# The down-projection of a two-layer encoder as seven block products, and the conv norm's transposes regrouped

## The chip, the core and the metric

The program runs on one core of a Trainium2 chip. Its metric is the device time of one execution in microseconds. The engines of the core run their own instruction streams and meet at semaphores: TensorE (PE, with weight loads shown as PEld), VectorE (DVE), ScalarE (ACT), GpSimd (POOL), and SyncE (SP), which here only issues transfers. ACT issues transfers too.

## What is computed

Two layers work on 1,024 prompt tokens and 256 sample tokens of width 1,024, all in float32. Layer 0 mixes tokens by a convolution module, layer 1 by windowed attention; each is followed by a gated feed-forward block of inner width 2,752 (21 tiles of 128 and a rest of 64):

```python
def conformer_conv(x, w_pw1, b_pw1, w_dw, b_dw, g_n, b_n, w_pw2, b_pw2):
    h = x @ w_pw1 + b_pw1
    a, gate = jnp.split(h, 2, axis=-1)
    h = depthwise_conv(a * jax.nn.sigmoid(gate), w_dw, b_dw)
    h = jax.nn.silu(layer_norm(h, g_n, b_n))
    return h @ w_pw2 + b_pw2
...
def conv_ffn(x, w_up, w_dw, b_dw, w_down):
    h = depthwise_conv(x @ w_up, w_dw, b_dw)
    g, u = jnp.split(h, 2, axis=-1)
    return (jax.nn.silu(g) * u) @ w_down
...
    for i in range(DEPTH):
        x = layer_norm(DEEPNORM_ALPHA * x + mix(x), ln_mix_g[i], ln_mix_b[i])
        x = layer_norm(DEEPNORM_ALPHA * x + conv_ffn(x, ...), ln_ffn_g[i], ln_ffn_b[i])
```

## The kernel before

The 1,280 tokens are ten row tiles of 128 (0 to 7 prompt, 8 and 9 sample). Every operand of a matrix product is split into a high and a low part, and `product` (L816) issues three matmuls for each product: high x high, low x high, high x low. Weights come in pieces of 128 rows and 512 columns: SP loads one into one of four slots of `raw_pieces`, ACT copies its high part into one of eight slots of `w_hi` once PE has used the piece eight before it, POOL subtracts to get the low part (`low`, L716), and only then is the raw slot free for SP.

The up-projection of the prompt already works by seven block products. It runs 21 sections (`sections`, L1072), one for each tile of the inner width; PE runs seven blocks of twelve matmuls of 512 columns and four of twelve of 256 columns for the sample tokens. During section f, ACT and POOL split the eight pieces of section f + 1, DVE makes the four sums of weights for them (`weight_sums`, L2054) and adds up the banks, ACT and DVE apply the width-3 convolution to tile f - 1 and f (`centre`, `tap`), and DVE multiplies gate and value (`hidden`, L2129). ACT then stores the tile of h into `h_dram` (`store_h`, L1607). There is one buffer, `up_out`, and `up_centre` (L1617) waits until the tile before it has been stored.

The down-projection reads h back. It runs three groups of row tiles (`D_GROUPS`: 0 to 3, 4 to 6, 7 to 9), each over 22 steps of the inner width; a step takes one part of h (four slots, split by ACT and DVE in `h_part`, L1548 and L2138) and two weight pieces (`down_step`, L1196): 24 matmuls in the first group, 18 in the others, and two thirds of that in the last step, where the 64 remaining rows of high and low part share one operand. At step 8 ACT queues the ten residual loads and the gains. After a group DVE adds its banks to the residual (`add_down`) and norms its tiles at steps 5, 8, 11 and 14 of the next group; in layer 1 POOL adds the shift (`add_shift`, L792) and SP stores the output. Behind layer 0 come the K, V and Q projections; their first eight weight pieces are split by POOL alone (`split` L665, `split_low` L675).

In the conv module PE turns the convolved tiles (`turn_conv`), ACT copies them out, DVE norms them, PE turns a normed tile back by eight transposes (`back_tile`, L896), ACT applies SiLU with gain and shift in eight pieces of 128 columns and copies the high part, DVE subtracts for the low part. The first projection (`out_projection`, L1019) waits for four tiles. Before that, `last_diagonals` (L1427) builds on ACT the diagonals of the last channel block's 32 taps.

## Time and profile before

| what | value |
|---|---|
| device time, median of three runs | 2,744.74 us (2,739.61 to 2,957.53) |
| device time of the profiled execution | 2,744.65 us |
| its span, first to last instruction | 2,742.8 us |
| PE busy | 2,646.5 us (96%) |
| DVE, ACT, POOL busy | 56%, 42%, 45% |
| bytes moved by DMA | 250.33 MB |

The profile is of one execution. Busy time of PE counts overlapping matmuls once; a matmul's own record is longer than the distance to the next one. "Idle before" in a row is how long the engine stood still ahead of the instruction, with the instruction that released it.

### The profile page before, as it was taken

The page shows a single profiled execution, that of the slowest core. Times are in us where ns is not written, and L with a number is a line of the kernel's source. Part 1 is how long each engine was busy: PE and PEld are TensorE (multiplying, and loading weights), DVE is VectorE, ACT ScalarE, POOL GpSimd, SP SyncE. Part 2 cuts the span into 40 slices and gives each one's busy share as a digit, 9 for nine tenths or more (in the row PEclk, how much of TensorE's full clock was granted, in tenths as well). Part 3 has the DMA queues.
Part 4 walks back from the last instruction along what each step waited for, and adds up shares of the span by engine and source line. Part 5 has one row for each costly group of instructions (what it writes and reads, how often), then busy time and mean ns, then how long its engine had stood idle before and what let it go on. Part 6 is the DMA issues. An engine that isn't in the chain of part 4 may idle for free.

```text
span 2742.8 us, 37236 instructions
## 1 busy us (share of the span) xinstructions
PE 2646.5 (96%) x13941; PEld 2175.6 (79%) x13941; DVE 1533.5 (56%) x2112; ACT 1164.4 (42%) x2247; POOL 1228.2 (45%) x939
## 2 busy tenths in 40 slices
PE   8999869989999999999999999998999999999996
PEld 7878757778888888888888754687888888888885
DVE  3598883975655565336640177458555555532543
ACT  3334543154444444334421288404444444443442
POOL 3212202454444444457643166436544444445775
PEclk9999989999999999999999999999999999999998
DMA  4000003222222223746532000422222222265563
GB/s 143 26 22 31 31 1 127 81 68 70 69 66 72 71 68 103 242 142 196 184 111 54 1 1 1 138 69 70 83 67 75 66 71 65 75 222 164 180 203 121
DMA packets 215295, 250.33 MB, mean 91 GB/s; under 512 B 34369, under 2 KB 153273, under 8 KB 215128
## 3 DMA queue, kind: packets, MB, share of 16 engines
q1 hardware_dynamic: 193736, 171.16, 20.9%
q10 hardware_dynamic: 21392, 76.95, 7.5%
q8 instruction: 104, 1.70, 0.3%
q14 instruction: 63, 0.52, 0.1%
HBM read 198.91 MB, written 49.15 MB: 90 GB/s over the span
## 4 chain that ended last, share of the span: by engine, by line
PE 87%; DVE 5%; ACT 3%; issue 3%; POOL 2%; DMA 1%; POOLq 0%; DVEq 0%; ACTq 0%; SPq 0%
PE bank L819 25%; PE bank L822 25%; PE bank L824 25%; PE bank L920 4%; PE bank L1287 2%; PE bank L1303 2%; PE bank L1315 2%; POOL w_lo L719 1%; ACT y L1491 1%; DVE y L1946 1%; DVE stats L1855 1%; PE bank L849 1%; DVE y L1869 0%; DVE s_lo L2047 0%; PE bank L866 0%
## 5 line engine op out<-in xcount | busy, mean ns | idle before, releaser
L719 POOL TENSOR_TENSOR w_lo<-raw_pieces,w_hi 128x512 fp32r<-128x512 f32 x564 | 791.8, 1413 | 721.3 <-ACT w_hi L1529 720.6
L1529 ACT ACTIVATE w_hi<-raw_pieces 128x512 fp32r<-128x512 f32 x564 | 351.6, 628 | 492.8 <-PE bank L819 418.6
L2147 DVE TENSOR_TENSOR h_lo<-h_raw,h_hi 128x384 fp32r<-128x384 f32 (+1 forms) x118 | 150.9, 1279 | 301.0 <-ACT h_hi L1555 301.0
L819 PE MATMUL bank<-w_hi,h_hi 128*128 128x512 f32 x776 | 303.2, 391 | 1.5 <-DVE y L2156 1.5
L824 PE MATMUL bank<-w_hi,h_lo 128*128 128x512 f32 x776 | 302.0, 389 | 0.0
L822 PE MATMUL bank<-w_lo,h_hi 128*128 128x512 f32 x776 | 301.9, 389 | 0.0
L673 POOL CAST w_hi<-raw_pieces 128x512 fp32r<-128x512 f32 x88 | 61.5, 699 | 492.2 <-PE bank L819 476.6
L819 PE MATMUL bank<-s_hi,w_hi 128*128 128x512 f32 x680 | 268.2, 394 | 3.9 <-ACT gate_rows L1579 3.9
L822 PE MATMUL bank<-s_lo,w_hi 128*128 128x512 f32 x680 | 265.8, 391 | 0.0
L824 PE MATMUL bank<-s_hi,w_lo 128*128 128x512 f32 x680 | 265.3, 390 | 0.0
L819 PE MATMUL bank<-x_hi,w_hi 128*128 128x512 f32 (+1 forms) x624 | 226.4, 363 | 1.6 <-DVE x_lo L1883 1.6
L824 PE MATMUL bank<-x_hi,w_lo 128*128 128x512 f32 (+1 forms) x624 | 221.7, 355 | 0.0
L822 PE MATMUL bank<-x_lo,w_hi 128*128 128x512 f32 (+1 forms) x624 | 221.6, 355 | 0.0
L1946 DVE SCALAR_TENSOR_TENSOR y<-glu,conv_table,y 128x1024 f32 (+3 forms) x266 | 215.6, 884 | 0.1
L819 PE MATMUL bank<-a_hi,w_hi 128*128 128x512 f32 x528 | 210.4, 399 | 4.1 <-DVE a_lo L2047 3.8
L822 PE MATMUL bank<-a_lo,w_hi 128*128 128x512 f32 x528 | 208.1, 394 | 0.0
L824 PE MATMUL bank<-a_hi,w_lo 128*128 128x512 f32 x528 | 206.7, 392 | 0.0
L819 PE MATMUL bank<-sample_hi,w_hi 128*128 128x256 f32 x688 | 194.2, 282 | 1.6 <-POOL w_lo L719 1.6
L824 PE MATMUL bank<-sample_hi,w_lo 128*128 128x256 f32 x688 | 194.7, 283 | 0.0
L822 PE MATMUL bank<-sample_lo,w_hi 128*128 128x256 f32 x688 | 194.6, 283 | 0.0
L819 PEld LDWEIGHTS bank<-w_hi,h_hi 128*128 128x128 f32 x776 | 145.7, 188 | 33.3 <-DVE h_lo L2147 2.3
L824 PEld LDWEIGHTS bank<-w_hi,h_lo 128*128 128x128 f32 x776 | 145.7, 188 | 30.3
(217 smaller groups left out, 5615.3 us busy)
## 6 DMA issues: line engine op xcount, KB each, us to landing
raw_pieces<-in_ffn_w_down_dram SPq DMA_DIRECT2D x252, 256.0 KB, 3.1
raw_pieces<-in_ffn_w_up_dram SPq DMA_DIRECT2D x168, 256.0 KB, 2.8
h_dram<-up_out ACTq DMA_DIRECT2D x42, 640.0 KB, 2.9
h_raw<-h_dram SPq DMA_DIRECT2D x84, 192.0 KB, 3.2
residual_dram<-y ACTq DMA_DIRECT2D x30, 512.0 KB, 2.6
y<-residual_dram ACTq DMA_DIRECT2D x30, 512.0 KB, 11.1
raw_pieces<-in_conv_w_pw_dram SPq DMA_DIRECT2D x48, 256.0 KB, 2.7
h_raw<-h_dram SPq DMA_DIRECT2D x34, 256.0 KB, 3.5
```

The costliest lines, as they stand in the source:

```text
L673: pool.tensor_copy(WH[:, ring(p), :], raw[:, r % RAW, :]).then_inc(piece_hi, 1)
L719: pool.tensor_tensor(WL[:, ring(p), :], source, WH[:, ring(p), :].bitcast(F32), ALU.subtract).then_inc(piece_split, 1)
L819: mm = pe.matmul(out, left[0], right[0], start=first, stop=False, skip_group_check=more)
L822: pe.matmul(out, left[0], right[1], start=False, stop=False, skip_group_check=more)
L824: return pe.matmul(out, left[1], right[0], start=False, stop=last, skip_group_check=more)
L920: mm = pe.matmul(bank[b + h][:, 0:n], diagonals[left][rows], right[rows, at:at + n], start=(first and m == 0), stop=(last and m == 2))
L1287: pe.matmul(bank[SCORE_BANKS[q % 3]][:, 0:len(kb) * P], q_sb[half, GROUP * rr + s // 2, cols(n)], k_sb[half, rr, kb[0] * P:(kb[-1] + 1) * ...
L1303: mm = pe.transpose(bank[PROBS_BANKS[u % 3]][:, cols(r)], probs_of(i)[:, 2 * r + par, c0:c0 + P], ident[:])
L1315: mm = pe.matmul(bank[AV_BANKS[i % 2]][par * HD:(par + 1) * HD, :], v_sb[:, kb[j], g * HD:(g + 1) * HD], probs_T_slot(i, j, par), start=(j ...
L1529: act.activation(WH[:, ring(base + p), :], source, ACT.Copy).then_inc(piece_hi, 1)
L1946: ins = dve.scalar_tensor_tensor(out=out, in0=glu[:, c, a0 + k:a0 + k + n], scalar=tap(k), in1=out, op0=ALU.mult, op1=ALU.add)
L2147: dve.tensor_tensor(out, landed_raw[0:rows, 0:n], hi[0:rows, 0:n].bitcast(F32), ALU.subtract).then_inc(h_low, 1)
```

## The change

For the prompt the down-projection becomes seven block products by pairs. Tiles 2m and 2m + 1 of h (m from 0 to 9), split at token 512, give four blocks of h; the matching rows of `w_down`, split at column 512, give four blocks of weights. Four sums of h blocks (POOL, in place, then stored by ACT to `s_dram`) and four sums of weight blocks (loaded by SP into `down_weights_*`, summed by POOL, stored by SP to `t_dram`) are made during the sections of the up-projection. `up_out` gets a second buffer. The down stage then runs eight phases of steps, each step one part of h, one weight piece and twelve matmuls into four banks; phases alternate between two sets of banks, DVE adds a set to the residual when its phase ends, and some phases go on accumulating in a set that has been added. The 21st tile and the rest are multiplied directly. The sample tokens follow in 22 steps with two weight pieces each. The norms run in the order 4 to 7, 0 to 3, 8, 9, at steps 69 to 91 of now 100.

In the conv module PE turns the normed tiles back four (then four, then two) at a time, one channel block k at a time, and SiLU, high and low part work on one k of 512 columns; the projection of a group starts with its first k. Half of the low diagonals are built ahead of ACT's wait for PE, and the high part of the last gate rows ahead of the last keeps.

The core of the diff (unchanged companions, semaphores and counts left out):

```diff
-    D_BANKS = [(4, 3, 2, 0, 7, 5, 1, 6), (4, 3, 2, 0, 5, 1), (4, 3, 2, 0, 5, 1)]
+    PAIRS_F = (FT - 1) // 2
 ...
+    PHASES = ("p2", "p7", "p1", "p4", "p6", "e22", "p5", "p3")
+    N_BLOCK = 7 * PAIRS_F + 8
+    H_ALL = N_BLOCK + H_STEPS
+    N_DOWN_PIECES = N_BLOCK + 2 * H_STEPS
 ...
+        DOWN = []
+        for phase, name in enumerate(PHASES):
+            m_all = range(PAIRS_F)
+            h_of = {"p2": [("h", 2 * m + 1, 0) for m in m_all], "p1": [("h", 2 * m, 0) for m in m_all],
+                    "p4": [("h", 2 * m + 1, HALF) for m in m_all], "p5": [("s", m, 0) for m in m_all],
+                    "p6": [("s", m, 1) for m in m_all], "p7": [("s", m, 2) for m in m_all],
+                    "p3": [("s", m, 3) for m in m_all], "e22": []}[name]
+            w_of = {"p2": [("w", 2 * m + 1, 0) for m in m_all], "p1": [("w", 2 * m, 0) for m in m_all],
+                    "p3": [("w", 2 * m + 1, 1) for m in m_all], "p5": [("t", m, 0) for m in m_all],
+                    "p6": [("t", m, 1) for m in m_all], "p7": [("t", m, 2) for m in m_all],
+                    "p4": [("t", m, 3) for m in m_all], "e22": []}[name]
+            if name in ("p2", "p4", "e22", "p3"):
+                t0, n = {"p2": (0, 0), "p4": (HALF, 0), "e22": (HALF, 1), "p3": (0, 1)}[name]
+                h_of += [("h", f, t0) for f in (FT - 1, FT)]
+                w_of += [("w", f, n) for f in (FT - 1, FT)]
+            for q, (h_from, w_from) in enumerate(zip(h_of, w_of)):
+                DOWN.append((phase, h_from, w_from, q == 0, q == len(h_of) - 1))
+        A_BANKS, B_BANKS, SMP_BANKS = (4, 3, 2, 0), (7, 5, 1, 6), (5, 1, 4, 0)
+        PHASE_BANKS = [A_BANKS if name in ("p2", "p1", "p6", "p5", "p3") else B_BANKS for name in PHASES]
+        PHASE_GOES_ON = [name in ("p4", "p6", "p5", "p3") for name in PHASES]
+        PHASE_SUMS = [{"p2": (0, 0), "p1": (0, 0), "p7": (4, 1), "p4": (4, 0), "p6": (4, 0), "e22": (4, 1),
+                       "p5": (4, 1), "p3": (0, 1)}[name] for name in PHASES]
+        PHASE_END = [max(i for i in range(N_BLOCK) if DOWN[i][0] == phase) for phase in range(len(PHASES))]
+        LN_ORDER = [4, 5, 6, 7, 0, 1, 2, 3, 8, 9]
+        LN_STEP = [69, 72, 75, 78, 82, 85, 88, 91]
 ...
+        def pieces_by(i):
+            return min(N_DOWN_PIECES, first_piece(i - 3) + 8) if i >= 4 else (3, 5, 6, 8)[i]
 ...
+                def down_piece(d):
+                    r, (kind, f, v) = base + RAWS_UP + d, piece_source(d)
+                    if kind == "t":
+                        for i in range(3):
+                            sp.wait_ge(w_stored[i], 16 * (layer + 1) * PAIRS_F * (2 if i == 0 else 1))
+                        row_piece(r, t_dram[f, v])
+                    elif f < FT:
+                        row_piece(r, down[cols(f), v * HALF:(v + 1) * HALF])
+                    else:
+                        slot_free(r)
+                        for s in range(2):
+                            sp.dma_start(raw[s * FR:(s + 1) * FR, r % RAW, :], down[FT * P:F, v * HALF:(v + 1) * HALF]
+                                         ).then_inc(raw_landed[r % RAW], 16)
+                for i in range(H_ALL):
+                    for d in pieces_of(i):
+                        down_piece(d)
+                    if i == 0:
+                        sp.wait_ge(ffn_x, UPS_X * layer + 4 * (FT - 1) + 2)
+                    if i == H_RING:
+                        sp.wait_ge(ffn_x, UPS_X * (layer + 1))
+                    if i >= H_RING:
+                        sp.wait_ge(h_low, H_ALL * layer + i - H_RING + 1)
+                    kind, f, v = h_source(i)
+                    rows, n = h_shape(i)
+                    if kind == "h":
+                        sp.wait_ge(*h_kept(layer, f))
+                        source = h_dram[f, 0:rows, v:v + n]
+                    else:
+                        sp.wait_ge(s_stored[v], 16 * PAIRS_F * (layer + 1))
+                        source = s_dram[f, v]
+                    sp.dma_start(h_slot(i)[0][0:rows, 0:n], source).then_inc(h_landed[i % H_RING], 16)
+                    if i == H_RING - 1:
+                        store_last_weight_sum(layer, PAIRS_F)
+                    if layer == 1 and i - 7 in LN_STEP:
+                        store_out(LN_STEP.index(i - 7))
 ...
+            def down_weight_sums(layer, f):
+                down, done, t0 = w["ffn_w_down"][layer], 16 * PAIRS_F * layer, 4 * PAIRS_F * layer
+                m = (f - 1) // 2
+                even, odd = cols(2 * m), cols(2 * m + 1)
+                if f % 2:
+                    if m == 0:
+                        sp.wait_ge(cell_turned, CELLS * (layer + 1))
+                        for t in (8, 9):
+                            sp.wait_ge(res_stored[t], 16 * (RES_FFN + 2 * layer))
+                    else:
+                        store_last_weight_sum(layer, m)
+                        sp.wait_ge(w_stored[1], done + 16 * m)
+                        sp.wait_ge(w_stored[2], done + 16 * m)
+                    sp.dma_start(wst[1][:], down[even, HALF:D]).then_inc(w_landed[1], 16)
+                    sp.dma_start(wst[2][:], down[odd, HALF:D]).then_inc(w_landed[2], 16)
+                    if m > 0:
+                        sp.wait_ge(w_stored[0], 2 * done + 32 * m)
+                    sp.dma_start(wst[0][:], down[even, 0:HALF]).then_inc(w_landed[0], 16)
+                else:
+                    sp.wait_ge(tsum_ready, t0 + 4 * m + 3)
+                    sp.dma_start(t_dram[m, 0], wst[0][:]).then_inc(w_stored[0], 16)
+                    sp.dma_start(t_dram[m, 2], wst[1][:]).then_inc(w_stored[1], 16)
+                    sp.dma_start(t_dram[m, 1], wst[2][:]).then_inc(w_stored[2], 16)
+                    sp.wait_ge(w_stored[0], 2 * done + 32 * m + 16)
+                    sp.dma_start(wst[0][:], down[odd, 0:HALF]).then_inc(w_landed[0], 16)
 ...
+            def s3(layer, m):
+                a11, a12, a21, a22 = h_halves(m)
+                pool.wait_ge(ffn_prod, H_STEPS * layer + 2 * m + 1)
+                if m == 0:
+                    pool.wait_ge(res_stored[8], 16 * (RES_FFN + 2 * layer))
+                    pool.wait_ge(cell_turned, CELLS * (layer + 1))
+                else:
+                    pool.wait_ge(s_stored[2], 16 * (PAIRS_F * layer + m))
+                pool.tensor_tensor(s3_rows[:], a11, a21, ALU.subtract).then_inc(hsum_ready, 1)
+            def s1(layer, m):
+                a11, a12, a21, a22 = h_halves(m)
+                pool.wait_ge(ffn_prod, H_STEPS * layer + 2 * m + 2)
+                pool.wait_ge(*h_kept(layer, 2 * m))
+                pool.wait_ge(hsum_ready, 4 * (PAIRS_F * layer + m) + 1)
+                pool.tensor_tensor(a21, a21, a22, ALU.add).then_inc(hsum_ready, 1)
+            def s2(layer, m):
+                a11, a12, a21, a22 = h_halves(m)
+                pool.wait_ge(hsum_ready, 4 * (PAIRS_F * layer + m) + 2)
+                pool.tensor_tensor(a11, a21, a11, ALU.subtract).then_inc(hsum_ready, 1)
+            def s4(layer, m):
+                a11, a12, a21, a22 = h_halves(m)
+                pool.wait_ge(*h_kept(layer, 2 * m + 1))
+                pool.wait_ge(hsum_ready, 4 * (PAIRS_F * layer + m) + 3)
+                pool.tensor_tensor(a12, a12, a11, ALU.subtract).then_inc(hsum_ready, 1)
 ...
+                for f in range(1, FT + 1):
+                    m = (f - 2) // 2
+                    sums = {} if f == 1 else {1: s3, 3: t1, 5: t3, 6: t2} if f % 2 == 0 else {1: s1, 2: s2, 4: s4, 6: t4}
                     for j in range(ROLES):
-                        role_low(layer, f, j)
-                for j, r in ((0, 0), (1, 1), (2, 0)):
-                    low(base + ROLES * FT + j, raw[:, (r0 + 4 * FT + r) % RAW, :])
-                for i in range(H_ALL):
-                    for n in range(2):
-                        low(base + N_UP + 2 * i + n, raw[:, (r0 + RAWS_UP + 2 * i + n) % RAW, :])
-                    g, f = divmod(i, H_STEPS)
-                    if layer == 1 and g >= 1 and f - 4 in LN_AT:
-                        before = D_GROUPS[g - 1]
-                        t = before[0] + LN_AT.index(f - 4)
-                        if t < before[1]:
-                            add_shift(t)
-            def add_shift(t):
+                        if f < FT:
+                            role_low(layer, f, j)
+                        elif j < 3:
+                            low(base + ROLES * FT + j, raw[:, (r0 + 4 * FT + (0, 1, 0)[j]) % RAW, :])
+                        else:
+                            down_low(j - 3)
+                        if j in sums:
+                            sums[j](layer, m if f % 2 == 0 else m)
 ...
+            def back_first():
+                pe.wait_ge(cn_ready, 4)
+                pe.wait_ge(ct_kept, TT)
                 for k in range(KT):
-                    mm = pe.transpose(bank[4 + 2 * (t % 2) + k // 4][:, cols(k % 4)], normed[:, t, cols(k)],
-                                      ident[:])
+                    for t in range(4):
+                        mm = pe.transpose(bank[k][:, cols(t)], normed[:, t, cols(k)], ident[:])
+                    mm.then_inc(cn_turned, 1)
+            def back_second(k):
+                pe.wait_ge(cn_ready, 8)
+                pe.wait_ge(silu_ready, k + 5)
+                for t in range(4):
+                    mm = pe.transpose(bank[4 + k % 4][:, cols(t)], normed[:, 4 + t, cols(k)], ident[:])
                 mm.then_inc(cn_turned, 1)
+            def back_third(m):
+                pe.wait_ge(cn_ready, TT)
+                pe.wait_ge(proj_kept, m + 1)
+                for k in (2 * m, 2 * m + 1):
+                    for t in range(2):
+                        mm = pe.transpose(bank[m][:, cols(2 * (k % 2) + t)], normed[:, 8 + t, cols(k)], ident[:])
+                mm.then_inc(cn_turned, 1)
+            BACK_AFTER = [{4: (0, 1, 2, 3), 5: (4,), 6: (5, 6), 7: (7,)}, {3: (0, 1), 4: (2, 3)}, {}]
+            def back_between(b, k):
+                for part in BACK_AFTER[b].get(k, ()):
+                    (back_second, back_third)[b](part)
 ...
+                def down_step(i):
+                    phase, h_from, w_from, first, final = DOWN[i]
+                    _, hi, lo = h_slot(i)
+                    p = base + N_UP + i
+                    pe.wait_ge(h_low, H_ALL * layer + i + 1)
+                    pe.wait_ge(piece_split, p + 1)
+                    weights = WH[:, ring(p), :], WL[:, ring(p), :]
+                    for j in range(4):
+                        out = bank[PHASE_BANKS[phase][j]][:]
+                        if first:
+                            down_bank_free(phase, j)
+                        if w_from[:2] != ("w", FT):
+                            mm = product(out, (hi[:, cols(j)], lo[:, cols(j)]), weights,
+                                         first and not PHASE_GOES_ON[phase],
+                                         final or h_from[:2] == ("h", FT - 1), uses=j == 3,
+                                         more=PHASE_GOES_ON[phase])
+                        else:
+                            mm = down_rest(out, hi[:, cols(j)], weights, j == 3)
+                        if final:
+                            mm.then_inc(down_done, 1)
+                    if not final:
+                        mm.then_inc(h_used, 1)
 ...
+                        if last and c == 1 and ch == 1:
+                            last_diagonals(1, 0, LAST_PAIRS // 2)
+                        if last and c == 1 and ch == 2:
+                            gate_high(c, i, last_glu[0])
 ...
+            silu(0, 0)
+            silu_high(0, 0)
+            silu(0, 1)
+            silu(0, 2)
+            silu(0, 3)
+            for k in range(4, KT):
+                silu_high(0, k - 3)
+                silu(0, k)
+            for k in range(KT - 3, KT):
+                silu_high(0, k)
 ...
                 def up_centre(f):
-                    if f >= 1:
-                        act.wait_ge(h_stored[f - 1], 16 * (layer + 1))
+                    m = (f - 2) // 2
+                    if f == 1:
+                        act.wait_ge(res_stored[8], 16 * stored)
+                    elif f >= 2:
+                        act.wait_ge(*h_kept(layer, f - 2))
+                        act.wait_ge(hsum_ready, 4 * (PAIRS_F * layer + m + 1))
+                        for part in ((0, 1), (3,))[f % 2]:
+                            act.wait_ge(s_stored[part], 16 * (PAIRS_F * layer + m + 1))
                     act.wait_ge(up_kept, KEPT_ALL * layer + 4 * f + 4)
                     act.wait_ge(up_summed, SUMMED_ALL * layer + 3 * f + 2)
-                    centre(up_out[:, 0:S0], up[:], f, 1)
+                    centre(up_out[f % 2][:, 0:S0], up[:], f, 1)
 ...
                     if i == 2 * H_RING:
-                        act.wait_ge(h_stored[FT - 1], 16 * (layer + 1))
-                        act.wait_ge(h_stored[FT], 16 * (layer + 1))
+                        act.wait_ge(*h_kept(layer, FT - 1))
+                        act.wait_ge(*h_kept(layer, FT))
+                        for part in range(4):
+                            act.wait_ge(s_stored[part], 16 * PAIRS_F * (layer + 1))
+                        for part in range(3):
+                            act.wait_ge(w_stored[part], 16 * PAIRS_F * (layer + 1) * (2 if part == 0 else 1))
                         for t in range(TT):
                             act.wait_ge(res_stored[t], 16 * stored)
                             act.dma_start(y[:, t, :], residual_rows[t]).then_inc(res_landed[t], 16)
                         load_gains(use, GAIN_ROWS[use])
 ...
+                    if i - 2 in PHASE_END:
+                        add_phase(PHASE_END.index(i - 2))
+                    if tile_at(i) is not None:
+                        down_stats(tile_at(i))
```

## Rows read from the trace of the kernel before

**Rows 1.** The head of the page, and busy time of each engine.

```profile
span 2742.8 us, 37236 instructions
...
PE 2646.5 (96%) x13941; PEld 2175.6 (79%) x13941; DVE 1533.5 (56%) x2112; ACT 1164.4 (42%) x2247; POOL 1228.2 (45%) x939
```

**Rows 2.** Windows: busy us of PE, PEld, DVE, ACT, POOL; clock; DMA share; GB/s.

```profile
637.00:662.00 25.00, 25.00 (x135) 21.66 (x134) 14.42 (x17) 11.57 (x18) 11.28 (x8) 1.00 0.22 69
1112.00:1137.00 25.00, 25.00 (x112) 20.72 (x111) 6.34 (x6) 8.03 (x14) 14.97 (x11) 1.00 0.86 299
...
2595.00:2620.00 25.00, 25.00 (x112) 20.69 (x111) 8.18 (x8) 11.07 (x19) 23.47 (x16) 1.00 0.65 207
```

**Rows 3.** Timeline of PE in the down-projection: start us, us, what.

```profile
1121.43 0.39 PE L819 MATMUL bank<-w_hi,h_hi 128*128 128x512 f32 x1
...
1128.23 0.39 PE L819 MATMUL bank<-w_hi,h_hi 128*128 128x512 f32 x1
...
1130.95 0.39 PE L819 MATMUL bank<-w_hi,h_hi 128*128 128x512 f32 x1
```

**Rows 4.** Timeline of POOL, two sections of the up-projection.

```profile
1013.00 1.42 POOL L719 TENSOR_TENSOR w_lo<-raw_pieces,w_hi 128x512 fp32r<-128x512 f32 x1 [3.41 <-ACT w_hi L1529]
1016.85 3.08 POOL L719 TENSOR_TENSOR w_lo<-raw_pieces,w_hi 128x512 fp32r<-128x512 f32 x2 [2.42 <-ACT w_hi L1529]
...
1041.71 3.10 POOL L719 TENSOR_TENSOR w_lo<-raw_pieces,w_hi 128x512 fp32r<-128x512 f32 x2 [2.41 <-ACT w_hi L1529]
```

**Rows 5.** Instructions of lines L737, L795, L2147: ns min/median/max, first and last start.

```profile
L737 POOL TENSOR_TENSOR y<-y x8: 1276/1290/1736, 524.8 to 1866.2; 128x512 f32<-128x512 f32 x8
...
L795 POOL TENSOR_TENSOR y<-y,shift_rows_end x10: 2331/2400/2730, 2572.4 to 2737.4; 128x1024 f32<-128x1024 f32 x10
...
L2147 DVE TENSOR_TENSOR h_lo<-h_raw,h_hi x118: 544/1340/1795, 1111.5 to 2703.9; 128x384 fp32r<-128x384 f32 x84, 128x512 fp32r<-128x512 f32 x34
```

**Rows 6.** Timeline of DVE, in the first section of rows 4.

```profile
1011.99 1.28 DVE L2101 SCALAR_TENSOR_TENSOR up_out<-up_rows,ffn_conv_table,up_out 128x1023 f32<-128x1023 f32 x1
...
1013.58 1.93 DVE L2101 SCALAR_TENSOR_TENSOR up_out<-up_rows,ffn_conv_table,up_out 128x1023 f32<-128x1023 f32 x1
...
1024.37 0.69 DVE L2064 TENSOR_TENSOR t_sum<-raw_pieces 128x512 f32<-128x512 f32 x1
```

**Rows 7.** Timeline of PE, first matmuls after two idle stretches of the convolution.

```profile
344.31 0.79 PE L920 MATMUL bank<-x_hi 64*128 64x512 f32 x2 [7.18 <-DVE x_lo L1924]
...
414.18 0.79 PE L819 MATMUL bank<-w_hi,x_hi 128*128 128x512 f32 x1 [8.06 <-DVE x_lo L2007]
```

**Rows 8.** Timeline of ACT, conv norm.

```profile
388.56 2.07 ACT L1478 ACTIVATE conv_normed<-bank 128x512 f32<-128x512 f32 x4 [0.27 <-PE bank L984]
...
395.97 1.28 ACT L1491 ACT_TABLE_LOAD   x1
397.27 2.90 ACT L1491 ACTIVATE y<-bank,channel_table 128x128 f32<-128x128 f32 x8
```

**Rows 9.** Timeline of ACT, last taps.

```profile
331.49 7.77 ACT L1432 ACTIVATE x_lo<-ident_half,last_tap_lo 128x64 fp32r<-128x64 f32 x32
```

**Rows 10.** Timeline of PE, the last matmul.

```profile
2721.18 0.39 PE L1217 MATMUL bank<-w_lo,h_hi 128*128 128x512 f32 x1
```

**Rows 11.** Timeline of ACT, first steps of layer 0's down-projection.

```profile
1110.81 0.62 ACT L1555 ACTIVATE h_hi<-h_raw 128x512 fp32r<-128x512 f32 x1
...
1122.47 5.95 ACTq L1740 DMA_DIRECT2D y<-residual_dram  x9
...
1129.02 1.00 ACTq L1367 DMA_DIRECT2D shift_rows_mid<-in_ln_ffn_b_dram  x1
```

**Rows 12.** DMA issues of the page: count, KB each, median us to landing.

```profile
raw_pieces<-in_ffn_w_down_dram SPq DMA_DIRECT2D x252, 256.0 KB, 3.1
```

**Rows 13.** Timeline of POOL, end of layer 0's down-projection.

```profile
1391.64 1.29 POOL L719 TENSOR_TENSOR w_lo<-raw_pieces,w_hi 128x512 fp32r<-128x512 f32 x1 [0.74 <-ACT w_hi L1529]
1393.04 0.78 POOL L673 CAST w_hi<-raw_pieces 128x512 fp32r<-128x512 f32 x1
```

511 lines of the change are left out of this document (286 added, 225 removed).

## The prediction

> **What bounds the kernel now.** I read the page first: the profiled execution has a span of 2,742.8 us inside 2,744.65 us of device time, and PE is busy for 96% of it [rows 1]. The table by windows then says how full each stage is: a section of the up-projection (25 us from 637) has PE busy for all 25.00 us at a granted clock of 1.00, the upper of its two levels (2.4 GHz), and so has the down-projection [rows 2]. So time comes out where matmuls go away, or in the few stretches where PE stands still. The timeline of PE prices a matmul: thirteen starts, twelve apart, from 1,128.23 to 1,130.95 are 2.72 us, that is 0.2267 us for 512 columns, not the 0.39 us that each record lasts [rows 3].
>
> The timelines of POOL and DVE show what would bound next. A section repeats after 24.86 us [rows 4]. A POOL subtraction of 512 columns takes 1.29 us alone [rows 5], the DVE tap of 1,023 columns 1.28 (1.20 net of the overlap with its neighbour). When they meet they take turns: POOL asked at 1,013.00 and took 1.42, because DVE's tap ran until about 1,013.2; DVE's next tap asked at 1,013.58, took 1.93 and ended 1.09 after POOL did [rows 4, 6]. Only DVE work with both inputs in SBUF shows this.
>
> **The change, part by part.**
>
> Matmuls. Of the prompt's down-projection 20 of the 21 full tiles of h are paired: 8 row tiles x 2 halves x 20 x 3 = 960 matmuls become 7 products x 10 pairs x 4 tiles x 3 = 840. The last full tile (48), the rest (32) and the sample tokens (260) stay. 120 fewer per layer, 240 in all, x 0.2267 = **-54.4**.
>
> Conv norm. PE's first projection starts at 414.18, after 8.06 us idle [rows 7]. ACT has kept the last conv tile at 390.6; it then loads a table (1.28) and makes SiLU a tile at a time, eight pieces of 128 columns in 2.90 [rows 8]; four tiles have to pass. Afterwards the first product needs one k of 512 columns: four transposes (0.5), table 1.28, SiLU, high and low part at about 0.6 each (ACT copies 512 columns in 0.62 [rows 11]; no row has SiLU at that width, which lies between 0.6 and the 1.45 that 4 x 0.36 would make): 390.6 + 0.5 + 1.3 + 1.8 = 394.4. Each further k costs ACT two such pieces, 1.2, against 2.72 on PE, so PE sets the pace from there on. The transposes (80 before and after) and the slow first matmuls (0.79 us for the first [rows 7]) are paid either way. 414.2 - 394.4 = **-19.8**; with SiLU at 1.45, -18.9; with a start held back by the second group's transposes, -16.
>
> Last taps. PE waits 7.18 us until 344.31, because ACT builds 32 diagonals for 7.77 us from 331.49 ahead of the last sigmoid [rows 7, 9]. Half of them now come before ACT's wait for PE at 328, and the high part of glu before the last keeps: 3.9 us earlier for the diagonals and about 1 for the keeps: **-4.8** (0 to -7.2).
>
> Tail. The last matmul starts at 2,721.18, 21.4 us before the span's end [rows 10]: three tiles are normed, now two. One tile's add, statistics and gain on DVE (3.5) and its POOL shift (2.4 [rows 5]) leave: 5.9, and one add less ahead of them (0.6): **-6.8** with the wait of DVE's last gain for POOL (-3.5 to -8).
>
> Up stage. POOL gets eight sums of 512 columns for each pair of tiles, four to a section: 1.29 us each by the nearest row, the same form [rows 5]. Before, the turns of a section are 8 x 1.28 on POOL and on DVE four wide taps at 1.20, the product over 1,280 columns at 1.5 and four weight sums at 0.6 [rows 4, 6]: 10.3 + 8.7 = 19.0. After: 24.1 of 24.86. It fits by 0.7 us. The waits it adds: POOL's s1 waits for the stored tile and for DVE's product, which is there some 2 us earlier; ACT's up_centre waits for two stores issued some 5 us earlier, of a kind that lands in about 3. Laid out in order, the worst delay is that DVE's second weight sum comes 1.6 us later, and ACT's keep behind it has 1.3 to 3 us to spare. SP's weight loads and stores fall between column pieces that POOL frees only later. Bounds: 0 (all hidden) to 50 (below); I take 0.1 us a section, **+4**.
> The Trainium skill (SBUF — State Buffer, "Who interferes with whom") says that DVE with two SBUF inputs and GpSimd hold that port pair exclusively, the second blocking until the first has finished. The 1.93 us above agrees. Were each engine counted alone, POOL would be busy for 15.4 of 24.86 us, and the sum would be 4 us less.
>
> Start of the down stage. A step is now 12 matmuls, 2.72 us, where it was 24 or 18. Layer 0's step 4 starts at 1,121.43 [rows 3], so the stage at 1,099.7; step 4 will want its h part at 1,110.6. But ACT, behind the last tile of h, splits part 4 only at 1,110.81 [rows 11], half a microsecond sooner after the change with one weight piece less in front; DVE, with a low of POOL before it, ends near 1,112.2: +1.6. Then ACT issues ten residual loads and two of gains; from the second of them at 1,122.47 to the last one's end at 1,130.02 are 7.6 us, with the first 7.9 [rows 11]. Before, steps of 5.44 us covered that; now the splits of step 8 are queued behind it, DVE's part behind these, and PE waits: +1.1. The loads (6.3 MB) run while SP asks 512 KB per 2.72 us, 193 GB/s, and before they already gave 299 GB/s at a DMA share of 0.86 [rows 2]; a weight piece otherwise lands in 3.1 us [rows 12]. Four h slots cover 10.9 us; 8 us of landing and 2 of splitting just fit, 10 do not: +2.8 (0 to 15). Two layers: **+11** (5 to 35).
>
> End of the down stage. In 22 sample steps of 2.72 us POOL has two lows (2.56) and DVE's part of 256 columns about 0.3 (544 ns is the shortest for 512 [rows 5]): 2.86. At most 8 pieces are ahead, so from the first sample step 36 lows, 18 parts and in layer 1 five shifts of 2.40 and four gains of 1.1 remain: 46 + 5 + 12 + 4 = 67 us, against 59 on PE; with a raw slot's round of 5.8 us for four pieces it is about the same. 67 + 1 for the last step, and some 2 of order: **+11** (5 to 25). Layer 0 has norms in place of shifts, 46 + 5 + 9 + 1 = 61, with 4 of order 65, against 63 on PE with its turns: **+2** (0 to 8).
>
> Behind it in layer 0 the K and V weights are split by POOL alone, a cast and a low from 1,393.04, after the last low at 1,391.64 [rows 13]: about 2.0 a piece, and K needs six: 12 us. They start when the last low is done. The ring lets that be 8 us before the end at best: +3.7; if POOL is late, +9. I take **+6**.
>
> Phase changes are costed at nothing: each bank set has another phase of at least two steps (4.5 us) between, against four adds of 0.65; from the seventh to the eighth phase each bank's add has 2.04 us. Splits per phase step (one low, one part) are 1.9 of 2.72. If that cover fails, each change costs at most the four adds, 2.6, in eight places a layer: 42.
>
> **The sum:** 2,744.65 - 54.4 - 19.8 - 4.8 - 6.8 + 4 + 11 + 11 + 2 + 6 = 2,692.9, say **2,693**. The profiled run is 0.1 us from the median of the three, 2,744.74.
>
> **Rivals.**
> All covers hold: only the forced pieces stay (5.4 at the two starts, 5 at the end of layer 1, 3.7 for K): 2,744.65 - 85.8 + 14 = 2,673. For it: PE never waited in the windows of layer 1 with POOL at 23.47 of 25 us [rows 2]. Against: a step is 2.72 us there, no longer 4.08. 0.20.
> The down stage starves on transfers: while 6.3 MB drain, SP gets half of 299 GB/s, 150 where 193 are asked, for 42 us: 12 a layer; and sample steps, 640 KB each with a 512 KB store in every third, ask 305 GB/s and take 3.2 us instead of 2.72: 11 a layer. In place of 2 x 2.8: 2,693 + 40 - 8 = 2,725. For: the 0.86. Against: the share falls again within two windows. 0.25.
> The up stage becomes bound by the shared turns (slower than before): 24.1 us of turns fill 24.86 only if under 3% is lost in order. With 10% lost a section takes 26.7, 1.8 more, x 40 = 72 in place of 4: 2,761. It decides from 1.4 us a section (26.3), where all of the gain is gone. For: 19.0 left 24% free before, and DVE and POOL wait for each other's results. Against: a late section finds PE's weights a section ahead. The exclusive hold is what the Trainium skill's page on SBUF (named above) states. 0.15.
> My forecast, 2,680 to 2,706: 0.40.
>
> **Numbers.** 0.8 of the chance lies from 2,670 to 2,744 (0.15 above, the rest below). 2% is about what a measurement of this kernel can tell from no change; 2% faster is under 2,689.9: all of the first rival and some 0.16 of the forecast, 0.36. Over 2% slower, above 2,799.6, is the end of the third rival: 0.04. Within 2%: 0.60.
>
> **What would show it.** 240 fewer matmul records and 13 starts still 2.72 us apart; the first projection near 394 and the first of the last taps near 339.5; sections still 24.9 us, with POOL busy near 17 of 25 us; gaps on PE in step 4 and 8 of each down stage, ended by DVE's h_lo; in the sample steps gaps ended by POOL's w_lo, most in layer 1; a gap before the first K projection ended by POOL; a tail of about 14.6 us. Sections of over 26 us would prove the sum wrong at its up term, a step rate over 3 us between phases at its transfer term.

## The result and the profile after

The changed kernel takes 2,728.79 us (median of 6 runs, 2,725.83 to 2,731.12), the kernel before 2,744.78: a ratio of 0.995, 95% interval 0.9938 to 0.9963. It is 16 us faster; 52 were forecast. The 2,957.53 us among the runs of the kernel before is a run in a slower state of the chip, which the ratio leaves out. The page of after, its head and the busy times, to be set against [rows 1]:

```profile
span 2726.3 us, 37914 instructions
...
PE 2601.9 (95%) x13701; PEld 2132.9 (78%) x13701; DVE 1744.7 (64%) x2226; ACT 1179.9 (43%) x2255; POOL 1513.8 (56%) x1079
```

240 matmuls are gone, as counted. But PE's busy time fell by 44.6 us only, where 240 x 0.2267 is 54.4, and PE now stands still for 124 us of the span where it was 96. So the matmuls went, and the time came back partly as waits and partly as matmuls that took longer.

Where, the PE timelines of both kernels tell, cut at five marks: the first matmul of each layer's down-projection, the first K projection, the last matmul, the end. "Forecast" adds up the terms of the prediction that fall into the stretch.

| stretch | before | after | difference | forecast |
|---|---|---|---|---|
| start to layer 0's down-projection | 1,099.67 | 1,079.42 | -20.3 | -22.6 |
| layer 0's down-projection to the first K projection | 305.73 | 318.24 | **+12.5** | **-13.7** |
| from there to layer 1's down-projection | 1,019.96 | 1,023.47 | +3.5 | +2.0 |
| layer 1's down-projection to the last matmul | 295.82 | 289.89 | -5.9 | -10.7 |
| last matmul to the end | 21.62 | 15.28 | -6.3 | -6.8 |
| sum | 2,742.8 | 2,726.3 | -16.5 | -51.8 |

26 of the 35 us that are missing lie in the second row. What PE waited for, from the view of waits of after over the whole execution (which line waited <- engine, tile and line that released it: us in total, times, longest):

```profile
PE bank L1037 <- DVE x_lo L2175: 19.6, 6, 5.9
PE bank L1006 <- POOL w_lo L796: 12.4, 7, 7.5
PE bank L1006 <- DVE h_lo L2441: 11.0, 9, 1.8
...
PE bank L1006 <- POOL w_lo L838: 8.0, 6, 2.0
```

The largest entry is in no term of the sum. L1037 is a transpose in `turn_tile`: a normed tile of layer 0, which PE turns for K, V and Q. The timelines of PE, DVE and ACT at one of them (start us, us, what, idle before and its releaser):

```profile
1286.67 1.63 PE L1037 MATMUL bank<-ident,y 128*128 128x128 f32 x8 [4.04 <-DVE x_lo L2175]
1287.95 0.78 PE L1006 MATMUL bank<-w_hi,h_hi 128*128 128x512 f32 x1
1288.53 0.63 PE L1009 MATMUL bank<-w_lo,h_hi 128*128 128x512 f32 x1
1288.95 0.63 PE L1011 MATMUL bank<-w_hi,h_lo 128*128 128x512 f32 x1
1289.38 0.63 PE L1006 MATMUL bank<-w_hi,h_hi 128*128 128x512 f32 x1
```

```profile
1278.56 2.31 DVE L2161 SCALAR_TENSOR_TENSOR y<-y,mean_var,gain_rows_mid 128x1024 f32<-128x1024 f32 x1
1280.79 0.15 DVE L2165 RECIPROCAL rstd<-std 128x1 f32<-128x1 f32 x1
1280.98 2.34 DVE L2167 SCALAR_TENSOR_TENSOR y<-y,rstd,shift_rows_mid 128x1024 f32<-128x1024 f32 x1
1283.24 1.28 DVE L2441 TENSOR_TENSOR h_lo<-h_raw,h_hi 128x512 fp32r<-128x512 f32 x2
1284.45 1.27 DVE L2147 BATCH_NORM_STATS2 stats<-y 128x6 f32<-128x512 f32 x2
1285.76 0.21 DVE L2150 BATCH_NORM_AGGREGATE mean_var<-stats 128x2 f32<-128x12 f32 x1
1285.88 1.24 DVE L2175 TENSOR_TENSOR x_lo<-bank,x_hi 128x512 fp32r<-128x512 f32 x2
```

```profile
1278.57 1.06 ACT L1618 ACTIVATE x_hi<-bank 128x512 fp32r<-128x512 f32 x2
```

All layer 0 tiles are turned into banks 6 and 7, so PE may turn a tile only when the low part of the tile before it has been taken out. ACT had the high part at 1,279.63. DVE took the low part from 1,285.88, because its order puts the next tile's norm (4.7 us), two h parts and the statistics of the tile after that first: PE turns a tile one step after the statistics, DVE takes the low part of the tile before behind an h part two steps further on. The two distances are as they were before; a step of that stage was 4.08 us, and PE waited 0.8 (the timeline of PE before):

```profile
1256.46 1.16 PE L849 MATMUL bank<-ident,y 128*128 128x128 f32 x8 [0.80 <-DVE x_lo L1883]
```

Two steps are now 5.4 us, 2.7 less than before: 0.8 + 2.7 = 3.5; the six waits are 1.4 to 5.9 us, 3.3 on average. The clock adds to it. After such a wait matmuls start 0.43 us apart (1,288.53, 1,288.95, 1,289.38) where [rows 3] has 0.2267. The windows of after (busy us of PE, PEld, DVE, ACT, POOL; granted clock; DMA share; GB/s):

```profile
1272.00:1290.00 18.00, 12.93 (x59) 10.37 (x58) 13.61 (x17) 6.05 (x12) 4.75 (x5) 0.92 0.45 145
...
1344.00:1362.00 18.00, 15.88 (x62) 12.93 (x63) 12.71 (x15) 7.67 (x16) 11.77 (x8) 0.78 0.58 179
```

From 1,272.3 to 1,397.66 PE waits 20.6 us at seven turns (19.6 for a low part, 1.0 for a norm) and 7.45 ahead of K:

```profile
1397.66 0.77 PE L1006 MATMUL bank<-x_hi,w_hi 128*128 128x512 f32 x1 [7.45 <-POOL w_lo L796]
```

352 matmuls at 0.2267 and 64 transposes at 0.14 (as before) are 88.8; the other 8.5 us of the 125.4 are a slower pace, most of it the lower clock.

### The profile page after: what moved, and what is told of

The parts are those of the page before. It is cut to its first block, busy times and chain, and to the rows that moved or that the text cites. A ratio compares the mean times of both kernels' runs of the same rounds, so it can differ in the third digit from the quotient of the medians.

```text
span 2726.3 us, 37914 instructions
## 1 busy us (share of the span) xinstructions
PE 2601.9 (95%) x13701; PEld 2132.9 (78%) x13701; DVE 1744.7 (64%) x2226; ACT 1179.9 (43%) x2255; POOL 1513.8 (56%) x1079
## 4 chain that ended last, share of the span: by engine, by line
PE 77%; DVE 10%; POOL 4%; issue 4%; ACT 3%; DMA 2%; ACTq 1%; POOLq 0%; DVEq 0%; SPq 0%
PE bank L1006 22%; PE bank L1009 22%; PE bank L1011 22%; PE bank L1130 3%; POOL w_lo L838 2%; PE bank L1528 2%; PE bank L1544 2%; PE bank L1556 2%; DVE y L2238 2%; DVE h_lo L2441 1%; DVE stats L2147 1%; DVE y L2161 1%; DMA h_raw<-h_sums_dram 1%; DVE y L2167 1%; PE bank L1037 1%
## 5 line engine op out<-in xcount | busy, mean ns | idle before, releaser
L838 POOL TENSOR_TENSOR w_lo<-raw_pieces,w_hi 128x512 fp32r<-128x512 f32 x544 | 826.3, 1528 | 473.6 <-ACT w_hi L1802 473.1
L1802 ACT ACTIVATE w_hi<-raw_pieces 128x512 fp32r<-128x512 f32 x544 | 339.2, 627 | 449.9 <-PE bank L1006 363.4
L2441 DVE TENSOR_TENSOR h_lo<-h_raw,h_hi 128x512 fp32r<-128x512 f32 (+1 forms) x182 | 229.7, 1272 | 190.4 <-ACT h_hi L1827 189.3
L1006 PE MATMUL bank<-w_hi,h_hi 128*128 128x512 f32 x728 | 290.0, 398 | 19.4 <-DVE h_lo L2441 11.0
L1009 PE MATMUL bank<-w_lo,h_hi 128*128 128x512 f32 x728 | 287.5, 395 | 0.0
L1011 PE MATMUL bank<-w_hi,h_lo 128*128 128x512 f32 x728 | 287.1, 394 | 0.0
L2399 DVE SCALAR_TENSOR_TENSOR gate_out<-gate_rows,ffn_conv_table,gate_out 128x1023 f32<-128x1023 f32 x88 | 153.1, 1739 | 62.5 <-ACT gate_out L1847 60.9
L1006 PEld LDWEIGHTS bank<-w_hi,h_hi 128*128 128x128 f32 x728 | 139.4, 191 | 55.4 <-DVE h_lo L2441 16.0
```

The lines of the kernel that those rows point to most:

```text
L838: pool.tensor_tensor(WL[:, ring(p), :], source, WH[:, ring(p), :].bitcast(F32), ALU.subtract).then_inc(piece_split, 1)
L1006: mm = pe.matmul(out, left[0], right[0], start=first, stop=False, skip_group_check=more)
L1009: pe.matmul(out, left[0], right[1], start=False, stop=False, skip_group_check=more)
L1011: return pe.matmul(out, left[1], right[0], start=False, stop=last, skip_group_check=more)
L1802: act.activation(WH[:, ring(base + p), :], source, ACT.Copy).then_inc(piece_hi, 1)
L2399: return dve.scalar_tensor_tensor(out=out[:, to], in0=source[:, at], scalar=column, in1=out[:, to], op0=ALU.mult, op1=ALU.add)
```

## The experiments

Two theories for layer 0 stood against each other, and a third beside them. **Order**: the place of the low part, at short steps. **DVE is full**: it is busy about 13 to 16 of 18 us there. **Weights**: POOL's low parts and K's pieces set the pace, as I had forecast. The edits are shown shortened.

**The parts of a turned tile earlier** (`e1_turn_early`). ACT and DVE:

```diff
-                    if layer == 0 and tile_at(i - 5) is not None:   # behind h_part(i)
+                    if layer == 0 and tile_at(i - 4) is not None:   # ahead of the pieces of step i
                         x_high(1, tile_at(i - 4))
                         store_residual(tile_at(i - 4))
-                    if layer == 0 and tile_at(i - 6) is not None:   # behind the norm
+                    if layer == 0 and tile_at(i - 4) is not None:   # ahead of h_part(i)
                         x_low(1, tile_at(i - 4))
```

> The changed kernel, but in layer 0 the high and low part of a turned tile are made by ACT and DVE two steps of h earlier (ACT ahead of the weight pieces of its step s + 4, DVE ahead of its h part s + 4, where s is the step of the tile's statistics). Theory A (order): PE waits 4 us for each turned tile because the low part that frees banks 6 and 7 stands on DVE behind an h part two steps ahead of PE's own place, and 2.72 us steps no longer cover a load of that part. Then the waits ended by x_lo (19.6 us) fall below 6 us and most of the 9 us lost at the lower granted clock comes back: 2,702 to 2,714 us. Rival B (DVE is full): DVE is busy 9 to 10 of 12 us there, a step's h part, norm and low parts need that much anyhow, so the waits only change their name, to DVE's y: 2,722 to 2,732 us. Rival C (weights): the stage is paced by POOL's low parts, 2.86 us a sample step, and by K's pieces: waits ended by w_lo take over, 2,718 to 2,728 us.

2,718.74 us, ratio 0.9914 (0.9896 to 0.9932): 10 us less than the change. The time lies between the first two theories and at the edge of the third's range, but the third has the wrong wait: those ended by `w_lo` grew by 1 us in all. The waits of this run:

```profile
PE bank L1006 <- POOL w_lo L796: 14.5, 7, 9.5
PE bank L1037 <- DVE y L2167: 13.0, 7, 2.9
```

No turn waits for `x_lo` any more: the order was the cause of those waits. But 13 us now wait for the norm of the tile itself, and K's wait grew from 7.45 to 9.5. Down-projection to K (the second row of the table): 308.1 us, from 318.2.

**The turn two steps later as well** (`e6_turn_late`).

```diff
-                    if layer == 0 and i - 1 in LN_STEP:             # PE, turn_tile
+                    if layer == 0 and i - 3 in LN_STEP:
-                    if layer == 0 and tile_at(i - 4) is not None:   # ACT and DVE, as in the run above
+                    if layer == 0 and tile_at(i - 6) is not None:
```

> The changed kernel; in layer 0 a normed tile is turned by PE three steps after its statistics in place of one, and its high and low part are made ahead of the splits of step s + 6. With the parts two steps earlier alone, the waits had changed from x_lo (19.6 us) to DVE's norm itself (13.0 us in seven waits): DVE still reached the norm of a tile only when PE stood at its turn. Theory (lead): DVE has time for all of it, what is missing is the distance between the norm and PE's turn; with two steps (5.4 us) more the waits fall below 3 us in all, and no low clock is left there: the stage from the first h product to the first K projection (305.5 us, 295.4 with the parts earlier) comes to 283 to 288 us, K's wait of up to 9.5 us still in it, 2,703 to 2,712 us. Rival (DVE is full): the norms push the h parts back, the waits are then ended by h_lo: over 293 us, 2,717 us or more.

2,716.12 us, ratio 0.9908 (0.9893 to 0.9924). From step 4, which is where the expectation begins to count (305.5 us in the changed kernel), it is 294.2 us to K, the rival's side, narrowly, and over my 288; by the table's marks it is 307.0, only 1.2 less than in the run above. The waits:

```profile
PE bank L1006 <- DVE h_lo L2441: 18.6, 13, 2.2
PE bank L1006 <- POOL w_lo L796: 15.0, 7, 10.0
```

No turn waits now; the h parts do (18.6 us over both layers, 11.0 in the changed kernel). So about 10 us of PE's time were the order of the low part. That DVE is full behind it is not shown: from 1,268 to 1,386 us DVE stands idle for 23.8 of 118 us, most of it for ACT's high part, while ACT stands idle for DVE's statistics (the views of waits of both engines in that window):

```profile
DVE h_lo L2441 <- ACT h_hi L1827: 19.4, 12, 2.7
```

```profile
ACT std L1612 <- DVE mean_var L2150: 47.3, 9, 7.7
```

ACT's order has a tile's standard deviation (`deviation`) ahead of the splits of the next step, so ACT holds its splits until DVE's statistics are done, and DVE then waits for the split. One such place is ahead of PE's wait of 1.84 us at 1,331.84:

```profile
1323.44 0.29 ACT L1612 ACTIVATE std<-mean_var,eps 128x1 f32<-128x1 f32 x1 [3.59 <-DVE mean_var L2150]
```

```profile
1325.12 0.79 DVE L2441 TENSOR_TENSOR h_lo<-h_raw,h_hi 128x256 fp32r<-128x256 f32 x1 [1.71 <-ACT h_hi L1827]
```

That is read from the trace; no run moves `deviation`. K's wait is 10.0 us: POOL's queue takes back a part (2.6 us) of what PE gained ahead of K.

**K's pieces first** (`e2_k_first`).

```diff
-            for j in range(4): column_piece(raw_of(B_KV + j), ...)        # V
-            for j in range(4): column_piece(raw_of(B_KV + 4 + j), ...)    # K
+            for j in range(4): column_piece(raw_of(B_KV + j), ...)        # K
+            for j in range(4): column_piece(raw_of(B_KV + 4 + j), ...)    # V
-    "... v 6, v 7, v 8, v 9, k 0.2, k 1.2"
+    "... v 6, v 7, k 0.2, k 1.2, v 8, v 9"
```

> The changed kernel, with the four pieces of K's weights loaded and split ahead of the four of V's (and the last two K products ahead of the last two V products). Theory (POOL's queue): PE's 7.45 us before the first K projection are six pieces split by POOL alone behind its last low part; now two pieces are enough, 4 x 2.0 us earlier: the wait falls under 1 us, 2,720 to 2,723 us. Rival (the chain of norms): the last tiles' norm, turn and low part end only little earlier, the wait is then ended by x_lo and at least 4 us of it stay: 2,725 to 2,729 us.

2,718.63 us, ratio 0.991 (0.9894 to 0.9927): 10 us, more than the wait of 7.45. Down-projection to K is 311.6 us (6.7 less), and 3.1 us more are saved behind it, up to layer 1's down-projection: in the changed kernel eleven matmuls behind the wait start 0.43 us apart and lose 2.7 us, here none does. POOL's queue of six pieces was the cause of the wait.

**Residual loads spread** (`e3_spread_loads`).

```diff
-                        for t in range(TT):                        # all ten ahead of the splits of step 8
-                            act.dma_start(y[:, t, :], residual_rows[t])
-                        load_gains(use, GAIN_ROWS[use])
+                    if 8 <= i < 13:                                # two behind the splits of each step
+                        for t in (2 * (i - 8), 2 * (i - 8) + 1):
+                            act.dma_start(y[:, t, :], residual_rows[t])
+                    if i == 14:
+                        load_gains(use, GAIN_ROWS[use])
```

> The changed kernel, with ACT's ten residual loads of the down stage issued two at a time behind its splits of steps 8 to 12 and the gains at step 14, in place of all twelve ahead of step 8. Theory (queue): PE's waits of about 2 us in either layer near step 8, ended by h_lo, come from the splits that stand behind 7.6 us of issues on ACT: they go, and layer 1's 2 us at a lower clock behind them; the 1.7 us at step 4 stay: 2,720 to 2,726 us. Rival (transfers): the loads drain at 390 GB/s with a DMA share above 1.0 whenever they are issued, the h parts land late all the same: 2,727 to 2,732 us.

2,724.78 us, ratio 0.9937 (0.9921 to 0.9954): 4 us, not clear of the spread by times alone, since the runs of both kernels overlap. Layer 0's stretch is 1.6 us shorter, layer 1's 3.0. In layer 0 PE's wait at step 8 (1.12 us) is gone: the queue on ACT was its cause. In layer 1 the wait that shrinks (1.79 us, to 0.6) stands at step 13, and there ACT waited for the transfer itself, an h part that SP had issued at 2,446.22, 12.3 us earlier (after):

```profile
2458.49 0.63 ACT L1827 ACTIVATE h_hi<-h_raw 128x512 fp32r<-128x512 f32 x1 [1.33 <-DMA h_raw<-h_sums_dram]
```

```profile
2459.90 0.50 PE L1006 MATMUL bank<-w_hi,h_hi 128*128 128x512 f32 x1 [1.79 <-DVE h_lo L2441]
```

While the residual loads drain, the windows of after from 1,099 and from 2,441 both have a DMA share of 1.04 and 391 GB/s. With the loads spread an h part still takes up to 14.1 us from its issue to ACT's copy (2,446.56 to 2,460.70); it is only issued earlier. So the rival holds in part: the queue and the transfers both have a share, and this run doesn't part them in layer 1.

**One part of the change at a time** (`conv_only`, `down_only`). The first is the kernel before with the conv norm's part of the diff (the last taps with it); the second is the changed kernel with that part taken back. PE's first projection in the changed kernel, which has 414.18 after 8.06 us of waiting in [rows 7]:

```profile
391.54 0.47 PE L1006 MATMUL bank<-w_hi,x_hi 128*128 128x512 f32 x1
```

> The kernel before with the conv part of the change alone (turning back by fours, the last diagonals earlier), the down-projection as it was. Theory (parts add up): the first section of the up-projection starts 20.7 us earlier, as between the two traces (594.5 to 573.8), and nothing after it changes: 2,724 us. That makes the seven products themselves worth only 5 us more. Rival (the conv part's gain depends on the down part or is given back at the K projections): 2,732 to 2,744 us.

> The changed kernel with the conv norm turned back tile by tile as before (the blocks of the out projection as the change has them). Theory: the down part alone does not pay for itself; its 54 us of matmuls are given back at the end of layer 0's down stage (27), in K's wait (7), at the two starts (11), at the end of layer 1 (15): from 2,743.5, at or above 2,743 us, up to 2,752. Rival (it pays, and the conv part is what disappoints): under 2,735 us.

`conv_only` takes 2,719.03 us, ratio 0.9916 (0.9899 to 0.9933): 24.4 us, not 20.7. `down_only` takes 2,751.63 us, ratio 1.0034 (1.0021 to 1.0047): without the conv norm's part the change makes the kernel slower by 9 us, and the whole gain is the conv norm's. The 3.7 us that the conv part is worth more alone have a cause that I had not seen: `conv_only` kept the out projection's blocks of tiles, 4, 2 and 4; the change has 4, 4 and 2. With two tiles in the last block a k takes PE 1.36 us and POOL's split of its weights 1.9, and PE waits for four of them (the first two, timeline of after):

```profile
455.83 0.50 PE L1006 MATMUL bank<-w_hi,x_hi 128*128 128x512 f32 x1 [0.88 <-POOL w_lo L796]
457.73 0.50 PE L1006 MATMUL bank<-w_hi,x_hi 128*128 128x512 f32 x1 [0.94 <-POOL w_lo L796]
```

`down_only` keeps the new blocks and has the same waits, 3.7 us in layer 0 and 1.3 in layer 1. So 5 of its 9 us are the blocks, and the seven products themselves cost about 4.

**How full is the shared port in the up-projection?** (`e4_two_more`, `e9_four_more`). Two, then four, of POOL's eight low parts of a section are made twice:

```diff
+                if f > 0 and j in (2, 5):              # e9: (0, 2, 5, 7)
+                    pool.tensor_tensor(WL[...], role_source(...), WH[...], ALU.subtract)
                 low(FFN_BASE[layer] + ROLES * f + j, role_source(...))
```

> The changed kernel, with two of POOL's eight low parts of each section of the up-projection made twice (the same values): 2 x 1.28 us more of POOL on the port that it shares with DVE. The sum of turns for the change was 24.1 us of a section's 24.86 and nothing was lost (sections 24.86 us). If the turns add up as counted, 26.7 us are wanted: sections of 26 us or more and 2,765 to 2,800 us. If the count is too high (DVE and POOL overlap more than counted), sections stay under 25.2 us: 2,729 to 2,740 us.

> The changed kernel, with four of POOL's eight low parts of a section made twice. With two, sections stayed at 24.86 us and POOL was busy for 24.7 of them by its records. If that is POOL's limit, four more operations in place of two make a section longer by most of 2.6 us: sections of 26.5 to 27.6 us, 2,800 to 2,850 us. If the busy time is largely waiting for the port that DVE gives back, sections stay below 25.5 us: under 2,765 us.

2,735.12 and 2,826.76 us (one run each). The windows of one section: of after, with two more, and with four more (each from its own start to the next section's):

```profile
677.60:702.46 24.86, 24.86 (x134) 21.51 (x133) 16.25 (x16) 11.60 (x17) 18.69 (x13) 1.00 0.39 126
```

```profile
684.30:709.16 24.86, 24.86 (x134) 21.52 (x133) 20.34 (x17) 11.80 (x17) 24.70 (x15) 1.00 0.40 126
```

```profile
689.30:716.53 27.23, 25.27 (x134) 21.38 (x133) 20.15 (x16) 11.57 (x17) 26.92 (x17) 1.00 0.36 111
```

Two more cost nothing in a section (of the 6 us by which the kernel is longer 4.3 lie in the first sections of layer 0; 2.4 lie ahead of the up-projection, where the two kernels are the same); four more make it 27.23 us. If POOL and DVE need 27.23 with four more, and each is 1.28, they need 22.1 with none, and 24.7 with two, which is POOL's busy time there. By this estimate my count of turns, 24.1, was 2.0 too high; which of the counted DVE operations let POOL pass, these runs don't show.

**No shift on POOL in layer 1** (`e5_no_shift`). The eight prompt tiles get the shift in two columns only.

```diff
-                pool.tensor_tensor(y[:, t, :], y[:, t, :], shift_end[:], ALU.add)
+                n = D if place >= 8 else 2
+                pool.tensor_tensor(y[:, t, 0:n], y[:, t, 0:n], shift_end[:, 0:n], ALU.add)
```

> The changed kernel; in layer 1 POOL adds the output's shift for the eight prompt tiles in two columns only (the rest of the shift is left out). Theory (POOL paces the sample steps of layer 1: two low parts of 1.28 us in each and a shift of 2.40 in every third, 10.1 us where PE wants 8.2): without the shifts PE's waits ended by w_lo (8.0 us, six, up to 1.98 each) go, and the clock lost behind them; from the first h product to the last, 277.2 us, comes to 267 to 271; 2,717 to 2,722 us. Rival (DVE, with gain, statistics and h parts, is as late): the waits change to h_lo, 274 us or more there, 2,725 to 2,730 us.

2,723.19 us (one run); from step 4 of layer 1 to the last matmul, 271.3 us from 277.2. The waits ended by POOL's `w_lo` at L838 fall from 8.0 us to two of 0.8, one in each up-projection, so POOL sets the pace of layer 1's sample steps. The waits of this run:

```profile
PE bank L1007 <- DVE h_lo L2442: 15.6, 14, 1.7
...
PE bank L1007 <- POOL w_lo L838: 1.6, 2, 0.8
```

Those for `h_lo` grew from 11.0 us. DVE is not full there either: from 2,640 to 2,706 it is busy for 30.7 of 66 us and stands idle for 33.7 until ACT's high part, while ACT stands idle for 18.3 us until weight pieces land and for 10.2 until DVE's statistics. Which of these is the next limit no run tests.

**All repairs together** (`e7_all`): the turns of `e6_turn_late`, K first, loads spread, and the old blocks, `BLOCKS = [(0, 4), (4, 6), (6, TT)]`.

> The changed kernel with four repairs: turns later and parts earlier in layer 0; K's pieces ahead of V's; residual loads two at a time; and the out projection's blocks of tiles as they were before (4, 2 and 4 tiles), since with a last block of two tiles PE waited 4 x 0.94 us for POOL's splits, which the conv part with the old blocks does not show. Sum by the stages: from 2,728.8, 3.6 for the blocks and 1.3 for them in layer 1, 17 to 25 for the turns, 7 to 9 for K, 4 for the loads: 2,687 to 2,697 us. Rival (the end of the down stage is bound by POOL, each repair uncovers the next wait): no more than 20 of it, 2,705 us or more.

2,695.96 us (2,692.6 to 2,698.36), ratio 0.9835 (0.9821 to 0.9848): 46 us under the kernel before, inside the sum of 2,687 to 2,697 and the fastest of all that ran. Its down-projection of layer 0 takes 294.95 us to K, 10.8 less than before, and layer 1's 287.92 to the last matmul. Against the change the first of these is 23.3 us shorter; K's wait is 6.9 of that and the loads 1.6, so the order of the turns is worth some 15 once POOL's queue takes nothing back. What PE still waits for, mostly in these two stretches:

```profile
PE bank L1006 <- DVE h_lo L2443: 15.8, 14, 2.0
...
PE bank L1006 <- POOL w_lo L838: 7.6, 6, 2.0
```

**Norms further apart** (`e8_norms`): the same with `LN_STEP = [67, 70, 73, 76, 80, 84, 88, 92]`.

> The kernel with the four repairs, with the tiles' statistics at steps 67, 70, 73, 76, 80, 84, 88, 92 in place of 69 to 91: the first four start right behind the addition of the seventh phase, the others are four steps apart in place of three. Theory (DVE is full over three steps: two wide norm operations of 2.1 to 2.3 us, statistics, a low part and three h parts are 10 us where PE takes 9.2): over four steps, 12.0 us of PE, it fits: the three waits of 1.9 us in layer 0 (ended by h_lo) go, and layer 1's shifts are spread further, 3 to 5 of its 5 us ended by w_lo go: 2,685 to 2,691 us. Rival (POOL and DVE lack time over the whole end, not in a place): 2,692 us or more.

2,702.96 us, ratio 0.9859 (0.9841 to 0.9877): no gain, 7 us more than `e7_all`. Layer 1's last stretch is 293.5 us, 5.6 more than in `e7_all`, and the waits for `h_lo` are longer (25.3 us, up to 3.4) while those for `w_lo` at L838 fall to 3.1. So it relieved POOL and hurt the h parts, and my reading that four steps give DVE room falls. At PE's longest wait (3.4 us, until 1,298.98) the trace has the same order as in `e6_turn_late`: ACT stands for DVE's statistics, then DVE for ACT's split:

```profile
1290.35 0.29 ACT L1612 ACTIVATE std<-mean_var,eps 128x1 f32<-128x1 f32 x1 [6.68 <-DVE mean_var L2152]
```

```profile
1291.72 1.36 DVE L2443 TENSOR_TENSOR h_hi<-h_raw,h_hi 64x512 fp32r<-64x512 f32 x1 [1.41 <-ACT h_hi L1827]
```

Whether that is why the h parts come later with the norms further apart is not settled.

## Why the prediction was right or wrong

- **Matmuls, -54.4.** Right: 240 fewer, and between 1,135 and 1,267 PE is busy without a gap; from the start of layer 0's down-projection to 1,272.3, 828 matmuls take 192.9 us, 5.2 more than at 0.2267.
- **Conv norm and last taps, -19.8 and -4.8.** The mechanism holds. The first of the last taps starts at 338.86 (344.31 in [rows 7]), the first projection at 391.54 (414.18): 22.6 together, 2 less than counted (the "near 394" among the prediction's signs leaves out the 4.8 of the taps; by its own sum the start is 389.6). Missed: the new blocks of tiles, +3.7 here and 1.3 in the out projection of layer 1.
- **Up-projection, +4.** Too high: sections stay at 24.86 us; the first one of layer 0 is 0.5 us late, layer 1's stretch some 1.7. The rival of the shared port is refuted for this kernel, and its limit measured: there was room for two more operations of POOL in a section, not for four. The Trainium skill (SBUF — State Buffer, "Who interferes with whom") has a DVE instruction with two SBUF inputs and a GpSimd instruction that reads SBUF contend for the shared port, which one of them holds to its end. The DVE norm operation at 1,278.56 in layer 0 agrees: it took 2.31 us beside a low part of POOL, where the same operation takes 1.27 at the least. The count of turns that I made did not come out.
- **Start of the down stage, +11.** The size is right: waits of 1.73, 1.12 and 0.94 us in layer 0, 1.70 and 1.79 in layer 1, with 1.4 and 2.5 at a slower pace: 5.2 and 6.0, where 5.5 each were forecast. Steps 4 and 8 of layer 0 are as costed (1.6 and 1.1), and the 1.79 us of layer 1 are the transfer term: landing took 12.3 us where 8 fit. But layer 1 has no wait at step 8; the 0.94 us stand behind DVE's additions of the first phase (2.47 us from 1,117.38), and phase changes were costed at nothing; and the 3.9 us at a slower pace were in no term. That the parts come to 11 is partly luck. Spreading the loads gives some 4 of the 11 back.
- **End of layer 0's down stage, +2: the step that failed.** I set POOL's sum (65 us) against PE's (63) and left DVE and the distances between the engines out. In place of 2 it took some 26: 20.6 us of waits and 8.5 at a slower pace, less the 3.2 us that PE waited there before. With the low part taken earlier the waits for it are gone (19.6 us to none, `e1_turn_early`), and the order is worth some 15 us in `e7_all`; the cause of the other 11, now mostly waits for h parts, stays open. I had written that the norms moved into short steps, costed what they add to POOL, and never asked what a distance of two steps, laid out for 4.08 us, covers at 2.72.
- **K and V splits, +6.** 7.45: right in place and size; by K first it is gone. The 2.7 us lost at the lower clock behind it were in no term.
- **End of layer 1, +11.** 12.1 us of waits and 4.1 at a slower pace, less 0.8 before: 15.4. The place and the engine were right (three waits of 1.97 to 1.98 and one of 0.47, ended by POOL's low part, 6.4 us in all); missing were DVE's additions of the last phase (1.14 and 0.76), four waits for h parts (3.8) and the pace.
- **Tail, -6.8.** -6.3.

Of the rivals, that all covers hold (2,673) failed at the same step as the forecast. The one in which the down stage starves on transfers gave 2,725, near the measured time, but by another way: while the loads drain, transfers stand behind one wait of 1.79 us where 12 a layer were set, spreading the loads gives back some 4 us in all, no wait of PE in the sample steps is ended by a transfer, and without POOL's shifts the steps get faster. ACT does wait 22.3 us for weight pieces in layer 1's sample steps of after, but they land 3.3 us after their issue; SP issues them late, since it waits 39.7 us there for POOL to free raw slots. The rival's sum doesn't close either: 12 and 11 a layer less 2 x 2.8 are 40, and the further -8 has no source; without it the rival stands at 2,733. It was the number only. The wide range (2,670 to 2,744) held the time, the forecast's own (2,680 to 2,706) did not; the gain of 52 did not come true mainly because of one stretch. With that stretch's order, K's queue, the loads and the blocks mended the kernel runs at 2,696, near the 2,693 of the sum. That nearness proves nothing: the repairs also take away some 10 us that the sum had counted for K and the loads, and the rest of that stretch's loss is still there.
